# Sums of output-projection weights: from VectorE in SBUF to adding DMA transfers in DRAM, with the low parts of three weight units moved from GpSimd to VectorE

## What is computed

```python
ua = jnp.einsum('blc,cd->bld', (oa.astype(x.dtype) * jax.nn.silu(za)), w_up_a)
ub = jnp.einsum('blc,cd->bld', ob * jax.nn.silu(zb), w_up_b)
merged = jax.nn.sigmoid(ga) * ua + jax.nn.sigmoid(gb) * ub
y = jnp.einsum('bld,de->ble', merged, w_out)
return layer_norm(ALPHA * x + y, ln_g, ln_b)
```

## Time and profile before

| | |
|---|---|
| median of 3 runs | 459.38 us (457.22 to 459.77) |
| the profiled execution's own time | 457.46 us |
| its span | 455.6 us, mean granted TensorE clock 0.996 |
| PE busy | 444.3 us (98%), 2946 matmuls |
| DVE busy | 318.9 us (70%) |
| ACT busy | 238.1 us (52%) |
| POOL busy | 190.0 us (42%) |
| DMA | 51.92 MB |

### The profile page before, as it was taken

How to read it: one execution, slowest core, us unless ns; L and a number is a source line. 1 busy time by engine, 2 the same in 40 slices (tenths; PEclk the granted TensorE clock), 3 DMA queues, 4 the chain that set the end, 5 groups by cost and what they waited for, 6 DMA issues and landing times.

```text
span 455.6 us, 7709 instructions
## 1 busy us (share of the span) xinstructions
PE 444.3 (98%) x2946; PEld 362.9 (80%) x2946; DVE 318.9 (70%) x583; ACT 238.1 (52%) x399; POOL 190.0 (42%) x177
## 2 busy tenths in 40 slices
PE   8999999999999999999999999999999999899893
PEld 7778888888888888888887887888788888788682
DVE  5446589999999854346989994880555048888976
ACT  5635445253345736294867565834774354434421
POOL 0444432583159813581004000000068495927964
PEclk9999999999999999999999999999999999999998
DMA  8808122256022720204120222032058734434013
GB/s 276 282 19 292 71 82 94 92 148 222 0 94 79 200 93 1 94 1 130 56 95 1 96 94 94 1 100 88 0 169 331 240 122 183 158 106 172 0 46 138
DMA packets 17299, 51.92 MB, mean 114 GB/s; under 512 B 2504, under 2 KB 4336, under 8 KB 16240
## 3 DMA queue, kind: packets, MB, share of 16 engines
q1 hardware_dynamic: 17024, 51.25, 33.5%
q10 hardware_dynamic: 240, 0.20, 0.2%
HBM read 46.18 MB, written 3.16 MB: 108 GB/s over the span
## 4 chain that ended last, share of the span: by engine, by line
PE 84%; DVE 10%; issue 3%; ACT 1%; DMA 1%; DVEq 0%
PE bank L648 21%; PE bank L649 21%; PE bank L650 21%; PE bank L796 2%; PE bank L811 2%; PE bank L894 2%; PE bank L847 2%; PE bank L978 1%; PE bank L980 1%; PE bank L981 1%; PE bank L787 1%; PE bank L786 1%; DVE mix L1754 1%; DVE s_lo L1780 1%; DVE bank L1750 1%
## 5 line engine op out<-in xcount | busy, mean ns | idle before, releaser
L2016 POOL TENSOR_TENSOR w_lo<-w_raw,w_hi 128x512 fp32r<-128x512 f32 x84 | 114.7, 1393 | 150.9 <-ACT w_hi L989 150.8
L648 PE MATMUL bank<-x_hi,w_hi 128*128 128x512 f32 x336 | 133.0, 396 | 0.0
L649 PE MATMUL bank<-x_lo,w_hi 128*128 128x512 f32 x336 | 131.1, 390 | 0.0
L650 PE MATMUL bank<-x_hi,w_lo 128*128 128x512 f32 x336 | 130.9, 390 | 0.0
L648 PEld LDWEIGHTS bank<-x_hi,w_hi 128*128 128x128 f32 x336 | 63.1, 188 | 13.8 <-issue 0.8
L650 PEld LDWEIGHTS bank<-x_hi,w_lo 128*128 128x128 f32 x336 | 63.1, 188 | 13.6
L649 PEld LDWEIGHTS bank<-x_lo,w_hi 128*128 128x128 f32 x336 | 63.1, 188 | 12.2
L989 ACT ACTIVATE w_hi<-w_raw 128x1024 fp32r<-128x1024 f32 (+2 forms) x63 | 62.4, 1013 | 7.3 <-PE bank L650 5.3
L1076 ACT ACTIVATE prob<-prob,nmax 128x128 f32<-128x128 f32 (+3 forms) x32 | 17.8, 557 | 41.5 <-DVE nmax L1535 41.4
L1511 DVE MAX8 best<-score 128x8 f32<-128x256 f32 (+2 forms) x48 | 26.8, 559 | 1.1
L1523 DVE COPY prob_t<-bank 128x128 f32<-128x128 f32 (+3 forms) x32 | 14.3, 486 | 19.0 <-PE bank L796 18.8
(11 more groups left out here) (271 smaller groups left out, 824.2 us busy)
## 6 DMA issues: line engine op xcount, KB each, us to landing
w_raw<-in_w_units SPq DMA_DIRECT2D x58, 512.0 KB, 4.7
z_b<-in_w_units SPq DMA_DIRECT2D x2, 1024.0 KB, 5.8
w_raw<-in_w_units SPq DMA_DIRECT2D x2, 1024.0 KB, 4.8
y_sb<-in_x_tok SPq DMA_DIRECT2D x4, 512.0 KB, 5.2
out<-y_sb SPq DMA_DIRECT2D x8, 256.0 KB, 2.0
x_raw_hi<-in_x_t SPq DMA_DIRECT2D x4, 256.0 KB, 4.6
x_raw_lo<-in_x_t SPq DMA_DIRECT2D x4, 256.0 KB, 5.6
t_turned<-t_row SPq DMA_DIRECT2D x1, 1024.0 KB, 9.7
```

The lines of the kernel that those rows point to most:

```text
L648: nc.tensor.matmul(dst, a_hi, b_hi, start=first, stop=False)
L649: nc.tensor.matmul(dst, a_hi, b_lo, start=False, stop=False)
L650: return nc.tensor.matmul(dst, a_lo, b_hi, start=False, stop=last)
L2016: nc.gpsimd.tensor_tensor(split_target(u, kiwi_lo, x_lo, w_lo)[:, k, :], raw(u)[:, k, :], split_target(u, kiwi_hi, x_hi, w_hi)[:, k, :].bi ...
```

## The change

1. t1 to t4 are no longer made by DVE. SP issues four DRAM-to-DRAM transfers of 1 MB that copy one block of each sum (just ahead of the loads of unit 17, `qa0`), and POOL issues four transfers with an adding write (`accum_op=ALU.add`, at q = 73, 76, 79, 84 of its program) that add the other block; t2 waits for t1's transfer and t4 for t2's. The sums are then loaded like any block. The scheme's signs change with it: t1 = b11 + b12, t2 = b22 + t1, t3 = b12 + b22, t4 = b21 + t2, and the row sums and three later operations of DVE take other signs.
2. `sum_rows` has three operations (one of 128x512, two of 128x256) where it had four of 128x256, and the first one waits for the last low piece of b21, since b21's raw buffer now lies over `s_raw` and `first_sum`.
3. b11, t1 and b21 are loaded together before `up0`; t1's place in `z_b` is as before. b21 is split at q = 110 (ACT high, POOL low), where it was 116 and 118; b11 is split at 109; the table load of ACT moves from 109 to 111. `t2_kept`, its store and the waits for it are gone, and `up1`'s loads no longer wait for DVE's sums.
4. The low parts of `up1`, `up2`, `up3` are made by DVE. All four low pieces of t1 are POOL's.
5. Semaphores of the last stores are merged into two (`y_done`), in the same order.

```diff
-LO_DVE = tuple(range(Q_PREP[0] // 4 + 1, Q_MERGE // 4 + 2))
-OUT_HI_AT = {109: ((0, 0),), 110: ((0, 1),), 120: ((2, 0), (2, 1))}
-OUT_HI_THEN = {116: ((1, 0), (1, 1))}
-OUT_LO_AT = {110: ((0, 0), (0, 1), (0, 2), (0, 3)), 118: ((1, 0), (1, 1), (1, 2), (1, 3)), 121: ((2, 2), (2, 3))}
-SUMS_AT, T1_LO_AT = 106, 121
+LO_DVE = (*range(Q_PREP[0] // 4 + 1, Q_MERGE // 4 + 2), *(UNITS.index(f"up{i}") for i in range(1, 4)))
+OUT_HI_AT = {109: ((0, 0), (0, 1)), 110: ((1, 0), (1, 1)), 120: ((2, 0), (2, 1))}
+OUT_LO_AT = {109: 0, 110: 1, 120: 2}
+OUT_SUMS = {"t1": ("b12", "b11"), "t2": ("b22", "t1"), "t3": ("b12", "b22"), "t4": ("b21", "t2")}
+Q_SUMS = {73: "t1", 76: "t3", 79: "t2", 84: "t4"}
...
-            with ExitStack() as s2:
-                early_sum = sb("early_sum", [P, PAIRS, SEQ], stack=s2)
...
+            with ExitStack() as s2:
+                b21_raw = sb("b21_raw", [P, PAIRS, SEQ], stack=s2)
             s_raw = sb("s_raw", [P, 4, HALF], stack=s)
             first_sum = sb("first_sum", [P, 2, SEQ], stack=s)
...
             for u in range(2, NMAIN):
-                if UNITS[u] == "up1":
-                    sp.wait_ge(out_sum, 2)
-                    sp.dma_start(t2_kept, early_sum[:]).then_inc(t2_saved, 16)
+                if UNITS[u] == "qa0":
+                    for name, (first, _) in OUT_SUMS.items():
+                        sp.dma_start(out_sums[name], out_block(first)).then_inc(sum_begun, 16)
                 if UNITS[u] == "up0":
                     sp.wait_ge(o_lo_done, 4)
-                    load_out("b11", z_a[:])
-                    load_out("b12", z_b[:])
-                    sp.dma_start(early_sum[:], out_block("b22")).then_inc(early_in_22, 16)
+                    for name in ("b11", "t1", "b21"):
+                        load_out(name)
...
             wait_out_lo(sp, 0, 4)
-            sp.wait_ge(t2_saved, 16)
-            sp.dma_start(z_a[:], t2_kept).then_inc(t2_in, 16)
+            load_out("t2")
             wait_lo(sp, UNITS.index("up2"), 4)
-            load_out("b21", out_raw("b21"))
+            load_out("b22")
             wait_lo(sp, UNITS.index("up3"), 4)
-            load_out("b22", out_raw("b22"))
+            load_out("t3")
             wait_out_lo(sp, 2, 4)
-            load_out("b12", z_b[:])
+            load_out("t4")
...
+                else:
+                    wait_out_lo(dve, 1, 4)
                 even, odd = mix[:, 0, :], mix[:, 1, :]
-                n = 4 * j
-                nc.vector.tensor_tensor(s_raw[:, 0, :], even[:, HALF:], odd[:, HALF:], ALU.add).then_inc(s_raw_done, 1)
-                nc.vector.tensor_tensor(s_raw[:, 2, :], even[:, 0:HALF], even[:, HALF:],
+                n = 3 * j
+                nc.vector.tensor_tensor(s_raw[:, 0:2, :], even.rearrange("p (i t) -> p i t", i=2), mix[:, :, HALF:],
                                         ALU.subtract).then_inc(s_raw_done, 1)
...
-                if q == SUMS_AT:
-                    sum_out("t1")
-                    sum_out("t2")
...
-            sum_out("t3")
             dve.wait_ge(ln_in, 32)
             rows_11(0)
-            sum_out("t4")
             rows_11(1)
...
+            def add_block(name):
+
+                first, second = OUT_SUMS[name]
+                pool.wait_ge(sum_begun, 16 * len(OUT_SUMS))
+                if second in OUT_SUMS:
+                    pool.wait_ge(sum_done[second], 16)
+                nc.gpsimd.dma_start(out_sums[name], out_block(second), accum_op=ALU.add,
+                                     max_dma_last_dim=8192).then_inc(sum_done[name], 16)
...
             for q in range(4 * NMAIN):
                 side(q)
-                for n, piece in OUT_LO_AT.get(q, ()):
-                    split_out_lo(n, piece)
-            for n in LO_ORDER[3:]:
+                if q in OUT_LO_AT:
+                    for piece in range(4):
+                        split_out_lo(OUT_LO_AT[q], piece)
+                if q in Q_SUMS:
+                    add_block(Q_SUMS[q])
+            for n in range(3, len(OUT_WEIGHTS)):
```

More of the change, by code:

```diff
@@ L254, in hybrid_kernel @@
                      "t3": c21_bank, "t4": c21_bank}
-        t2_kept = nc.dram_tensor("t2_kept", [P, PAIRS, SEQ], F32).ap()
+        out_sums = {n: nc.dram_tensor(f"out_{n}", [P, PAIRS, SEQ], F32).ap() for n in OUT_SUMS}
         t5_row = nc.dram_tensor("t5_row", [HEADS_B, T5W], F32).ap()
@@ L308, in hybrid_kernel @@
         ln_scaled, ln_mult = sem("ln_scaled"), sem("ln_mult")
-        y_done = [[sem(f"y_done{t}_{half}") for half in range(2)] for t in range(TB)]
+        y_done = [sem("y_done_dve"), sem("y_done_pool")]
         rounds = topk_rounds()
@@ L478, in out_raw, with wait_y_done @@
         def out_raw(name):
[L480 to L484, removed]
+            if name in ("b22", "t3"):
+                u = UNITS.index({"b22": "up2", "t3": "up3"}[name])
+                return w_raw[:, u % 2, :].rearrange("p (j n) -> p j n", j=PAIRS)
+            return {"b11": z_a, "t1": z_b, "b21": b21_raw, "t2": z_a, "t4": z_b}[name][:]
         def out_block(name):
-            return w_units[NMAIN - 1 + OUT_BLOCKS.index(name)].rearrange("p (j n) -> p j n", j=PAIRS)
+            if name in OUT_BLOCKS:
+                return w_units[NMAIN - 1 + OUT_BLOCKS.index(name)].rearrange("p (j n) -> p j n", j=PAIRS)
+            return out_sums[name]
         def wait_out_raw(eng, name):
[L491 to L498, removed]
-        def wait_out_lo(eng, n, pieces):
[L502 to L510, removed]
+            eng.wait_ge(out_in[name], 16)
+        def wait_out_lo(eng, n, pieces):
+            eng.wait_ge(out_lo, 4 * n + pieces)
         def wait_out_hi(eng, n, half):
-            eng.wait_ge(out_hi, 2 * HI_ORDER.index(n) + half + 1)
+            eng.wait_ge(out_hi, 2 * n + half + 1)
         def wait_y_full(eng, name, i):
             eng.wait_ge(y_full, OUT_ORDER.index((OUT_WEIGHTS.index(name), i)) + 1)
+        def wait_y_done(eng, t, half):
+            on_pool = half in ON_POOL[t]
+            order = [(v, h) for v in range(TB) for h in range(2) if (h in ON_POOL[v]) == on_pool]
+            eng.wait_ge(y_done[on_pool], order.index((t, half)) + 1)
         def m_part(m):
@@ L537, in out_stationary @@
                 return hi[:, c], lo[:, c]
-            k = {"t1": 0, "t2": 1, "t3": 2, "b22": 3}[name]
+            k = {"t3": 0, "t1": 1, "t2": 2, "b22": 3}[name]
             return s_part(s_hi, j)[:, k, c], s_part(s_lo, j)[:, k, c]
@@ L639, in _ @@
                     c = slice(half * 512, half * 512 + 512)
-                    sp.wait_ge(y_done[t][half], 1)
+                    wait_y_done(sp, t, half)
                     sp.dma_start(out[t][:, c], y_sb[:, t, c]).then_inc(y_out, 16)
@@ L1376, in _ @@
                     round_merged(m)
-                for n, half in OUT_HI_THEN.get(q, ()):
-                    split_out_hi(n, half)
-                if m is not None and m % 2:
-                    round_sums(m // 2)
+                    if m % 2:
+                        round_sums(m // 2)
             split_out_hi(3, 0)
@@ L1842, in rows_12 @@
                 dve.wait_ge(early_12, i + 1)
-                nc.vector.tensor_tensor(c12_bank[i][:], c12_bank[i][:], u_sum[:, i, :], ALU.add).then_inc(pre_12, 1)
+                nc.vector.tensor_tensor(c12_bank[i][:], c12_bank[i][:], u_sum[:, i, :], ALU.subtract).then_inc(pre_12, 1)
             def rows_22(i):
@@ L1861, in normalise_half @@
                 nc.vector.scalar_tensor_tensor(out=y_sb[:, t, c], in0=y, scalar=rstd[:, t, 1:2], in1=ln_gb[:, 1, c],
-                                               op0=ALU.mult, op1=ALU.add).then_inc(y_done[t][half], 1)
+                                               op0=ALU.mult, op1=ALU.add).then_inc(y_done[half in ON_POOL[t]], 1)
             def normalise(t):
```

56 lines of the change are left out of this document (16 added, 40 removed).

## The result

The changed kernel took 454.64 us (median of 5, 454.04 to 455.05) against 457.66 us (median of 5, 457.22 to 459.77) for the kernel before in the same comparison: ratio 0.9918, 95% interval 0.9895 to 0.994. The profiled executions are 454.26 (span 452.4) and 457.46 (455.6): 3.2 us less. Later runs qualify this: both kernels have executions on two levels (medians 457.30 and 459.40 for the one before, 454.63 and 458.83 for the changed one), and the changed kernel's five all fell on its lower one, which was luck. Over all executions timed or profiled, 17 of the changed kernel and 70 of the one before, the means are 455.85 and 458.43, 2.6 us (0.56%) apart. Where the levels come from is the second half of this study.

What follows compares the result with a forecast made beforehand. TensorE was taken as the bound, busy 444.3 of 455.6 us, with gains only where it stands still. 3.8 us won less 0.95 and 0.2 gives 2.65; 459.38 - 2.65 = 456.7 us, range 454.5 to 459.7.

Steps and rivals of the forecast that it cites:

- The sum: Whole kernel: 3.8 us won, 0.95 lost to new stops, 0.2 to slower restarts, a gain of 2.65 us.
- behind PE's last matmul nothing changes: Last rows and stores, 448.6 to 455.6 us: same operations, so no gain there.
- The tail: PE's second stop, near 431 us: t3 and t4 leave DVE's queue, the stop goes entirely, 2.4 us.
- The up projections: `up0` to `up3`: POOL's penalties on DVE go, but DVE's added low pieces make two small PE stops.
- The two new stops: PE waits for late merges at part 4 (0.5 us) and part 6 (0.45 us).
- The cover of "one microsecond": At `sum_rows(0)`: POOL done with b21 at 377.4, DVE there at 378.45, so the wait costs nothing.
- The first rival: DVE bounds the up projections; two missed locks leave a gain of 0.4 us, 459.0; chance 0.28.
- I take nothing here too: Adding transfers beside unit 21's load: cost 0, the load landing near 261 and wanted at 264.53.
- the bound of 10: Upper bound of 10 us for one adding transfer of 1 MB, from two reads and a write; lower 3.3.
- the second rival: Adding transfers hold up unit 21's load, landing 5.7 us late; up to 462.4 us; chance 0.08.
- the signs of being wrong: PE stop over 1.5 us at part 4 or 6, or any between 200 and 340, among others.
- The third rival: Up projections: DVE and ACT half a microsecond earlier, no new stops, all 3.8 us won, 455.6; chance 0.12.

Runs made afterwards that it cites:

- the edit alone: Kernel before without DVE's sums t3 and t4 (t3 read from b12's buffer, t4 from b21's): 455.06 us, ratio 0.9935.
- the run with the low parts alone: Kernel before with the low parts of `up1` to `up3` made by DVE, nothing else changed: 462.95 us, ratio 1.0101.

## Why the prediction was right or wrong

**The sum held, its reference didn't.** The forecast was 456.7 us, the measured median 454.64, 2.06 less. Level against level the change is worth 457.30 - 454.63 = 2.67 us; the forecast had 2.65. The step that failed is the last one of the sum, "the median of the three runs lies 1.92 above that execution, and against it the forecast is 459.38 - 2.65": two of those three executions lay on the longer level, where the profile of one such execution shows the clock fallen behind the second stop. That isn't a shift that carries over to the changed kernel, since the change takes the very stop away. In about half of its executions the kernel before loses not 2.4 but 4.5 us at that stop. The hint was there: the three times (457.22, 459.38, 459.77) form two groups, and the profiled execution (457.46) belongs to the lower one. Against it the prediction's own sum gave 454.8. The measured 454.64 lies in the range, near its lower end.

That the sum agrees to 0.02 us is partly luck. In the two profiled executions 2.97 us were won between the first matmul of `up0` and the last start, where 2.65 were forecast, and 0.3 behind it, where nothing was ("behind PE's last matmul nothing changes"). Their spans are 3.2 us apart, the medians of the levels 2.67. So in most executions the changed kernel must reach `up0` some half a microsecond later than the one before, which is worked out and not seen: in the four profiled short executions of the kernel before that moment varies from 362.63 to 363.17, and in the one of the changed kernel it is 363.24. The transfers don't explain it, since without them `up0` begins at 363.38 and the median is 454.48.

**The tail.** As forecast: no wait on L1843 is left, `rows_12` waits for PE instead, and the edit alone gives 2.3 us of the 2.4. b22's low parts weren't late.

**The up projections.** The two new stops were forecast at 0.95 with 0.2 for restarts, and measured 0.52 with 0.32: right in place and cause, a third too large. The chain of sums started 0.26 us earlier than taken (378.19 for 378.45) and the rest ran as worked out: pieces from 379.70, a wait of 0.87 for ACT, `merge(2)` at 383.07 (383.3), `merge(4)` at 394.43 (394.7). The run with `up2` rounded together shows that the wait for ACT was the term that decided. The cover of "one microsecond" for the wait for b21's last piece was half of that in the measured execution: POOL ended at 377.7 and DVE came at 378.19. With the pieces back on POOL the cover is gone, and DVE stands 2.43 us.

**The first rival** (DVE becomes the bound) did not come, but the missed locks that it names are real: in the run with the low parts alone they come at POOL's pieces of b21, with 4.2 us of stop.

**The transfers.** "I take nothing here too" was right for what it named and failed for what it didn't. Copies: 16 us, cost nothing. The Trainium skill (DMA: Bandwidth & Descriptors, Latency and other measured facts) gave an estimated 20 us; the trace shows 16 to the last landing, and 452 GB/s from 164 to 169 us, which is faster than its rate. Adding transfers: 8.2 to 13.6 us each against the bound of 10. The Trainium skill (Collectives: The Full Stack, The bandwidth ceiling) has an add need two source reads and so half the rate, an estimated 7 us; the trace is near that for t1 and t3 together, 7.1 us a megabyte, and t4's, the only one with no other adding transfer beside it from issue to landing, took 8.2:

```profile
out_t<-out_t POOLq DMA_DIRECT2D x1, 1024.0 KB, 8.2
```

Unit 21's slack held, by 0.8 us. An adding transfer that holds something up, as in the second rival, did come in 5 of 17 executions, but on a queue that no row group of mine contained: that of the instructions. Among the signs of being wrong, "any stop of PE between 200 and 340" is the one that came. Its price is 4.2 us, its mean here 5/17 x 4.2 = 1.2. The second rival had 0.08 and named the wrong victim.

**The third rival** (no new stops, 455.6) described the edited version: with `up2` rounded together they are gone.

**The version that beats both** is that one with the adding transfers at 212 us: 453.49 us, all five executions within 1 us, ratio 0.9889 [0.9867, 0.991]. The one with t3's adding transfer later (453.5) can't be told from it; the early one has a DMA share of 0.77 from 212 to 247 us, where the instruction packets are far apart.

## What to carry to other kernels

Before you subtract from a median, see which level it stands on. Here two levels 0.5% apart were, in the kernel before, a stop of TensorE that sometimes costs its clock as well, and the change that removed the stop removed the gamble with it. When a transfer that fills the DMA engines is added, list everything that shares them, the instruction queue of the page's part 3 included, and try the transfer where TensorE's instructions are long, not where hundreds of short ones go by: here that took the long executions from 5 of 12 to none of 16. One profile of a short execution proves a cost absent only from that execution; enough timed ones to see the spread are needed besides.

## What was not expected of the hardware

- Instructions arrive by DMA in pieces of 16 KB (23 in an execution), and one that was 5.8 us late beside adding transfers went with a stop of TensorE of 2.75 us.
- A stop of 1.9 us is followed by a granted clock of 0.50 in some executions (37 of 70, going by their times) and by 1.00 in others; 2.75 and 4.2 us were followed by it in executions profiled here, though one with 2.75 us (the kernel with three times the copies) kept 1.00:

```profile
260.00:265.00 5.00, 3.04 (x21) 1.00 1.05 236
```

- 1 MB added in DRAM lands 8.2 to 13.6 us after its issue, where a load of 1 MB into SBUF (b11) took 4.8, and a load issued beside it lands 11 to 14.5 us after its issue instead of some 5.
